# Hybrid decoder trunk on one core: stage boundaries by token blocks, halved norms, an early third gain load, a 512-column first gather and a turned dense product

## What is computed

```
for layer in range(2):
    h = rmsnorm(x, ln1_g[layer])
    a_u, a_b, a_c, s_u, q, k, v, qi, ki, wi, gates = split_columns(h @ w_in[layer])
    y_a = short_conv_mixer(a_u, a_b, a_c, conv_w[layer]) @ w_out_a[layer]
    y_b = s5_mixer(s_u, ...) @ w_out_b[layer]
    y_c = dsa_mixer(q, k, v, qi, ki, wi, ...) @ w_out_c[layer]
    g = sigmoid(gates)                       # three gates of width 1024
    mixed = g[0] * y_a + g[1] * y_b + g[2] * y_c
    x = x + mixed @ w_o[layer]
    h2 = rmsnorm(x, ln2_g[layer])
    x = x + (swiglu(h2, w1, w3, w2) if layer == 0 else moe_ffn(h2, router_w, w1, w3, w2))
```

## Time and profile before

| | us |
|---|---|
| median of 3 runs | 1764.49 (1762.76 to 1767.69) |
| time of the profiled execution | 1763.59 |
| its span from first to last instruction | 1761.8 |
| PE busy | 1687.8 (96%) |
| DVE busy | 1369.3 (78%) |
| ACT busy | 1061.5 (60%) |
| POOL busy | 427.0 (24%) |

### The profile page before, as it was taken

The page is one execution under the profiler, slowest core; times in us unless marked ns, Lnnn a source line. Parts: engine busy times, 40 slices in busy tenths (PEclk is TensorE's granted clock), DMA queues, the critical chain, the costliest instruction groups (busy, mean ns, idle before and its releaser), DMA issues.

```text
span 1761.8 us, 24272 instructions
## 1 busy us (share of the span) xinstructions
PE 1687.8 (96%) x8960; PEld 1431.0 (81%) x8960; DVE 1369.3 (78%) x1135; ACT 1061.5 (60%) x860; POOL 427.0 (24%) x537
## 2 busy tenths in 40 slices
PE   7899998999979999979999999999999999999998
PEld 5887877999868878768888888888888888888886
DVE  6989575454459886558888888888888888888887
ACT  5443455544343544437777777777777777777775
POOL 8979400999024352020000000000000000000200
PEclk9999999999989999979999999999999999999999
DMA  9433365556443343638999999999999999999995
GB/s 326 122 118 116 125 203 176 178 192 200 152 156 121 117 149 129 206 119 293 389 358 388 370 378 386 370 369 382 371 373 378 375 374 389 362 382 369 385 395 193
DMA packets 212425, 481.53 MB, mean 273 GB/s; under 512 B 7904, under 2 KB 32608, under 8 KB 212112
## 3 DMA queue, kind: packets, MB, share of 16 engines
q1 hardware_dynamic: 207456, 463.34, 73.7%
q0 software_dynamic: 4480, 16.78, 2.6%
q10 hardware_dynamic: 432, 0.65, 0.1%
HBM read 473.40 MB, written 7.34 MB: 273 GB/s over the span
## 4 chain that ended last, share of the span: by engine, by line
PE 85%; DVE 10%; ACT 2%; issue 1%; DMA 1%; DVEq 0%; SPq 0%; ACTq 0%; POOLq 0%
PE ps L632 25%; PE ps L634 25%; PE ps L633 25%; DVE w_lo L277 3%; PE ps L1086 1%; PE ps L656 1%; PE ps L657 1%; PE ps L658 1%; ACT w_hi L272 1%; PE ps L755 1%; PE ps L780 1%; PE ps L698 1%; PE ps L782 1%; PE ps L757 1%; DMA raw<-w_in 1%
## 5 line engine op out<-in xcount | busy, mean ns | idle before, releaser
L277 DVE TENSOR_TENSOR w_lo<-raw,w_hi 128x2048 fp32r<-128x2048 f32 (+1 forms) x439 | 1012.1, 2313 | 271.0 <-ACT w_hi L272 269.8
L272 ACT ACTIVATE w_hi<-raw 128x2048 fp32r<-128x2048 f32 (+1 forms) x439 | 839.4, 1914 | 418.7 <-PE ps L634 399.8
L632 PE MATMUL ps<-w_hi,xg_hi 128*128 128x512 f32 x896 | 355.9, 397 | 1.8 <-issue 1.4
L634 PE MATMUL ps<-w_hi,xg_lo 128*128 128x512 f32 x896 | 350.2, 391 | 0.0
L633 PE MATMUL ps<-w_lo,xg_hi 128*128 128x512 f32 x896 | 349.7, 390 | 0.0
L632 PE MATMUL ps<-w_hi,hT_hi 128*128 128x256 f32 (+2 forms) x672 | 229.0, 341 | 2.2 <-DVE hT_lo L1627 2.2
L633 PE MATMUL ps<-w_lo,hT_hi 128*128 128x256 f32 (+2 forms) x672 | 225.3, 335 | 0.0
L634 PE MATMUL ps<-w_hi,hT_lo 128*128 128x256 f32 (+2 forms) x672 | 225.0, 335 | 0.0
L632 PE MATMUL ps<-w_hi,hidT_hi 128*128 128x512 f32 x536 | 209.7, 391 | 3.0 <-DVE hidT_lo L1949 3.0
L634 PE MATMUL ps<-w_hi,hidT_lo 128*128 128x512 f32 x536 | 208.8, 390 | 0.0
L633 PE MATMUL ps<-w_lo,hidT_hi 128*128 128x512 f32 x536 | 208.6, 389 | 0.0
(11 more groups left out here) (357 smaller groups left out, 2046.4 us busy)
## 6 DMA issues: line engine op xcount, KB each, us to landing
raw<-moe_w SPq DMA_DIRECT2D x336, 1024.0 KB, 7.2
raw<-w_in SPq DMA_DIRECT2D x44, 1024.0 KB, 5.5
raw<-ffn_w SPq DMA_DIRECT2D x33, 1024.0 KB, 5.2
raw<-w_o SPq DMA_DIRECT2D x8, 1024.0 KB, 4.9
...
```

What stands on the lines that cost most here:

```text
L272: act.activation(w_hi[:, n % SPLIT, 0:width], raw[:, n % RAW, 0:width], ACT.Copy).then_inc(hi_done, 1)
L277: dve.tensor_tensor(w_lo[:, n % SPLIT, 0:width], raw[:, n % RAW, 0:width], w_hi[:, n % SPLIT, 0:width].bitcast(F32), ALU.subtract).then_in ...
L632: pe.matmul(dst, x_hi, hi, start=first, stop=False, skip_group_check=True)
L634: return pe.matmul(dst, x_lo, hi, start=False, stop=last, skip_group_check=True)
```

## The change

1. **Token blocks at the stage boundaries.** Turned banks now hold one token block and four channel tiles each (`turned_ps`), so a block's bank is complete without the other block. `w_o` is worked as: chunk 0 for block 0, transposes of `mixed` block 1, chunk 0 for block 1, chunk 1 whole, then `two_rows`: the last two chunks for block 0, then for block 1 by column halves. PE turns `mixed` block 0 ahead of the last quarter. Norm steps 1 to 3 run through `enter`: block 0 complete ahead of block 1, and the second of the two early chunk splits moves behind them. The turned banks are 4 to 7 where the addition reads 0 to 3 and the reverse. C_KV goes to banks 4 and 5, with its first half by blocks.
2. **Norm by halves.** Additions, squares and scales work on 512 columns. A dummy root (`root_table`) loads its table before the norm's first square.
3. **Third norm's weights.** Gain 2 is loaded into `su` after the last merge of mixer 0, no longer into `gate` at norm 2.
4. **First gather.** 8 matmuls of 512 columns bring expert 0's rows into `xg_tok`, 8 transposes turn them, in two halves, with copies by ACT and DVE between.
5. **Dense product turned.** `up` has weight tiles stationary and 256 tokens moving, so `hid` comes out turned; `turn_hidden` is gone, and `hid` is split from SBUF. The last stripe's split goes to `h_hi`/`h_lo`, and its `rows` joins `two_rows`. The loop's last pair is written out. The four clearing matmuls of banks 4 to 7 come after the first `up`.

The core of the diff (a line of "..." where lines are left out):

```diff
+        def turned_ps(bank, b, half):
+            return ps[:, bank + 2 * b + half, :].rearrange("p (k n) -> p k n", k=4)
...
+            def two_rows(n, xs, bank, parts, second_ready=None):
+                tile = lambda n, k, h: lambda w: slot_view(w, n, (2, D))[:, k, h * HALF:(h + 1) * HALF]
+                for i, (x_hi, x_lo, k0) in enumerate(xs):
+                    if i == 1 and second_ready is not None:
+                        pe.wait_ge(S["hidT_lo_done"], second_ready)
+                    pe.wait_ge(lo_done, n + i + 1)
+                    for k in range(2):
+                        for h in range(2):
+                            mm = three(ps[:, bank + h, :], x_hi[:, k0 + k, 0:P], x_lo[:, k0 + k, 0:P], n + i,
+                                       tile(n + i, k, h), False, i == 1 and k == 1)
+                mm.then_inc(parts, 1)
+                for h in range(2):
+                    for i, (x_hi, x_lo, k0) in enumerate(xs):
+                        for k in range(2):
+                            mm = three(ps[:, bank + 2 + h, :], x_hi[:, k0 + k, P:SEQ], x_lo[:, k0 + k, P:SEQ], n + i,
+                                       tile(n + i, k, h), False, i == 1 and k == 1)
+                        if h == 1:
+                            mm.then_inc(used, 1)
+                        elif i == 1:
+                            mm.then_inc(parts, 1)
...
+            def turn_block(src, b, bank, ready, seen, done):
+                for k in range(KD):
+                    if k % 4 == 0:
+                        pe.wait_ge(ready, seen + k // 4)
+                    at = (k % 4) * P
+                    tr = pe.transpose(ps[:, bank + 2 * b + k // 4, at:at + P], src[:, b, k * P:k * P + P], ident[:, :])
+                    if k % 4 == 3:
+                        tr.then_inc(done, 1)
+            def norm_turn(i, b, bank):
+                turn_block(h_tok, b, bank, S["h_done"], 4 * i + 2 * b + 1, S["hT_ps"])
...
+            def out_quarters(n, k0, x_hi, x_lo, layer):
+                pe.wait_ge(lo_done, n + 1)
                 for b in range(BLOCKS):
-                    for k in range(KD):
-                        if k % (KD // parts) == 0:
-                            pe.wait_ge(ready, seen + parts * b + k // (KD // parts) + 1)
-                        at = (k % 2) * SEQ + b * P
-                        tr = pe.transpose(ps[:, bank + k // 2, at:at + P], src[:, b, k * P:k * P + P], ident[:, :])
-                        if b == BLOCKS - 1 and k % 2:
-                            tr.then_inc(done, 1)
-            def norm_turn(i):
-                turn_rows(h_tok, 0, S["h_done"], BLOCKS * i, S["hT_ps"])
+                    tok = slice(b * P, b * P + P)
+                    for h in range(2):
+                        for k in range(2):
+                            mm = three(ps[:, 2 * b + h, :], x_hi[:, k0 + k, tok], x_lo[:, k0 + k, tok], n,
+                                       lambda w: slot_view(w, n, (2, D))[:, k, h * HALF:(h + 1) * HALF], False, k == 1)
+                        if (b, h) == (1, 1):
+                            mm.then_inc(used, 1)
+                        else:
+                            mm.then_inc(S["ob_quarters"], 1)
+                        if (b, h) == (1, 0):
+                            turn_block(mixed, 0, 4, S["mixed_done"], 5 * layer + 2, S["mixT_ps"])
...
+                columns_block(c0 + C_KV, 4, 0, 4, KV_W, 0)
+                if layer == 1:
+                    norm_turn(2, 1, 0)
+                    turn_b(1)
+                pe.wait_ge(S["hT_lo_done"], 8 * layer + 3)
+                columns_block(c0 + C_KV, 4, 0, 4, KV_W, 1)
...
+                rows_block(c0 + C_WO, 0, hT_hi, hT_lo, 0, True, False)
+                turn_block(mixed, 1, 4, S["mixed_done"], 5 * layer + 4, S["mixT_ps"])
+                pe.wait_ge(S["mixT_lo_done"], 4 * layer + 3)
+                rows_block(c0 + C_WO, 0, hT_hi, hT_lo, 1, True, False).then_inc(used, 1)
+                rows(c0 + C_WO + 1, 2, hT_hi, hT_lo, False, False)
+                pe.wait_ge(S["mixT_lo_done"], 4 * layer + 4)
+                two_rows(c0 + C_WO + 2, ((hT_hi, hT_lo, 4), (hT_hi, hT_lo, 6)), 0, S["x_parts"])
...
+                        hi, lo = (slot_view(w, n + which, (KD, DENSE_W)) for w in (w_hi, w_lo))
                         for k in range(KD):
                             if i is None and which == 0 and k == KD // 2:
                                 pe.wait_ge(S["hT_lo_done"], 8)
-                            for b in range(BLOCKS):
-                                tok = slice(b * P, b * P + P)
-                                mm = three(ps[:, bank, b * DENSE_W:(b + 1) * DENSE_W], hT_hi[:, k, tok],
-                                           hT_lo[:, k, tok], n,
-                                           lambda w: slot_view(w, n + which, (KD, DENSE_W))[:, k, :],
-                                           k == 0 and b == 0, k == KD - 1)
+                            for c in range(DENSE_W // P):
+                                dst = ps[:, bank, c * SEQ:(c + 1) * SEQ]
+                                cols = slice(c * P, (c + 1) * P)
+                                pe.matmul(dst, hi[:, k, cols], hT_hi[:, k, :], start=k == 0 and c == 0, stop=False,
+                                          skip_group_check=True)
+                                pe.matmul(dst, lo[:, k, cols], hT_hi[:, k, :], start=False, stop=False,
+                                          skip_group_check=True)
+                                mm = pe.matmul(dst, hi[:, k, cols], hT_lo[:, k, :], start=False, stop=k == KD - 1,
+                                               skip_group_check=True)
...
+                norm_turn(1, 0, 4)
+                norm_turn(1, 1, 4)
+                pe.wait_ge(S["hT_lo_done"], 7)
+                up(n0, None, 0)
                 pe.wait_ge(S["zero_made"], 1)
                 clear(4, 4)
...
+                stripe(pairs - 1, 0)
+                up(n0 + 5, DENSE_STRIPES - 1, pairs - 1)
+                pe.wait_ge(S["hidT_lo_done"], DENSE_STRIPES - 1)
+                two_rows(n0 + DENSE_CHUNKS - 2, ((x_hi, x_lo, 0), (last_hi, last_lo, 0)), 4, S["x_parts"],
+                         DENSE_STRIPES)
...
+                def first_gather():
+                    pe.wait_ge(S["pick_done"], BLOCKS)
+                    for half in range(2):
+                        cols = slice(half * HALF, (half + 1) * HALF)
+                        for b in range(BLOCKS):
+                            for src in (h_hi, h_lo):
+                                mm = pe.matmul(ps[:, 2 + half, :], pick[:, b, :], src[:, b, cols],
+                                               start=b == 0 and src is h_hi, stop=b == 1 and src is h_lo,
+                                               skip_group_check=True)
+                        mm.then_inc(S["first_rows"], 1)
+                    for k in range(KD):
+                        if k % 4 == 0:
+                            pe.wait_ge(S["first_taken"], k // 4 + 1)
+                        tr = pe.transpose(ps[:, 6 + k // 4, (k % 4) * P:(k % 4) * P + P],
+                                          xg_tok[:, k * P:k * P + P], ident[:, :])
+                        if k % 4 == 3:
+                            tr.then_inc(S["gather_ps"], 1)
...
+            def root_table():
+                act.wait_ge(S["consts"], 1)
+                act.activation(norm_ss[:, 6, 0:1], ones[:, 0:1], ACT.Sqrt)
...
+                    root_table()
+                    norm(2, 0)
+                    turned_hi(2, 0, S["hT_ps"], 0, S["hT_hi_done"])
+                    norm(2, 1)
                     sp(1)
-                    norm(2)
...
                 split_hi(act, n)
+                root_table()
+                norm(1, 0)
+                turned_hi(1, 0, S["hT_ps"], 4, S["hT_hi_done"])
+                norm(1, 1)
                 split_hi(act, n + 1)
-                norm(1)
...
+                def made_hi(i, rows_used):
+                    act.wait_ge(S["hid_done"], i + 1)
+                    if rows_used is not None:
+                        act.wait_ge(used, rows_used)
+                    act.activation(hidT_hi[:, :], hid[:, :], ACT.Copy).then_inc(S["hidT_hi_done"], 1)
...
+            def enter(i, bank, after, gains, turned_bank):
+                add(i, 0, 0, bank)
+                add(i, 0, 1, bank)
+                variance(i, 0)
+                scale(i, 0, gains)
+                add(i, 1, 0, bank)
+                add(i, 1, 1, bank, after)
+                turned_lo(i, 0, S["hT_hi_done"], turned_bank, S["hT_lo_done"])
+                variance(i, 1)
+                scale(i, 1, gains)
+                turned_lo(i, 1, S["hT_hi_done"], turned_bank, S["hT_lo_done"])
...
+                merge_last(layer, 0)
+                merge_last(layer, 1)
+                merge_last(layer, 2)
+                turned_lo(layer, 0, S["mixT_hi_done"], 4, S["mixT_lo_done"])
+                merge_last(layer, 3)
```

(10 more changed lines are left out.)

363 lines of the change are left out of this document (204 added, 159 removed).

## The result

The changed kernel takes **1746.41 us** (median of 4 runs, 1745.96 to 1747.2) against 1764.09 for the kernel before, run beside it (4 runs). The ratio is 0.9897, 95% interval 0.9885 to 0.9909. The prediction was 1745, range 1738 to 1753. The profiled execution took 1746.7 us, 16.9 less than the one of before.

The account below looks back on a forecast made before the run. PE, busy 96% of the span, was taken as the bound, so only its idling, turning or half clock could be won. Terms summed to -19.2 from 1763.6, giving 1744.4; with 0.9 for the median, 1745 us, range 1738 to 1753.

Parts of the forecast that it names:

- The turned product: Dense FFN: same matmul rate, removed transposes save 3.8 us in the steady loop, 0.9 in the first stripe, 2.0 at the end.
- The clock term of the entry: Entry into the dense FFN after the first norm: some half clock now lies over product, +0.6 us, between 0 and 1.7.
- The merges: End of each mixer: new order loses 0.6 us each; 1.4 given back in layer 1 for half clock; sum -0.2.
- Norm 1: Entry into the dense FFN: block 0 is ready when PE ends its product, gain 2.05 us.
- norm 2: Entry into mixer 1: early gain row and C_KV's start by blocks gain 8.8 us, between 4.3 and 9.5.
- norm 3: Ahead of routing, to the logits' copy: gain only 0.3 us, as the moved chunk split and two `h_lo` stand between.
- Table loads: Norms: the early root puts loads before the squares, in idle time; at the kernel's start 0, between -0.6 and +1.3 us.
- The gather: First gather, before the experts: halves gain 2.3 us; PE starting nearer the low-clock stretch costs +0.6 (0 to 1.2).
- (a): Rival: four or five more half-clock stretches on product, over two merges and three norm entries, giving 1753 us; chance 0.13.
- (b): Rival: ACT or DVE order eats the overlap; of norms 1 to 3 only the gain row's 4.3 us is left, 1752; chance 0.08.
- (c): Rival: the turned dense product runs slower because weight loads show between matmuls, 1770 to 1787 us; chance 0.03.
- (d): Rival: the gain row or freed transposes were hidden anyway, nothing moves by over 5 us, 1761 us; chance 0.04.

Follow-up runs that it names:

- the one just told: Changed kernel with four edits (low half before weight split, chunk 32 behind merge, shifted count, early squares): 1734.96 us, ratio 0.9829 to the kernel before.
- the single edit: Kernel before, with only the third norm's weights loaded early, into `su` behind the last merge of mixer 0: 1760.75 us, ratio 0.9976.

## Why the prediction was right, and where it was wrong

**The bound.** "What is won ahead of the experts arrives at the end unreduced" held: the experts' time lies between 970.9 and 971.6 in nine profiles in which their first product runs at full clock, whatever came before; the tenth is the one just told. (One of the nine has the shorter period.)

**The turned product.** -3.8 -0.9 -2.0 = -6.7 was near on the kernel before (-6.6, with 1.7 of unplanned waits in it), and its rate was 286 ns as before. In the changed kernel the dense product won 3.0. The step that failed is "`hidT_lo` has a whole `up` (11.5 us) to arrive; 0". The product it feeds is late if the low half is, and the low half has not a whole `up`: on DVE it stands behind the split of chunk m+1, which itself waits for ACT's part. And it now reads two SBUF tiles, where the form before read one PSUM bank and one tile. All instructions of the two forms (ns min, median, max): those of the kernel before in its dense stage, eight of which overlap one of POOL's longer instructions, then those of the changed kernel in the experts and in the dense stage:

```profile
L1949 DVE TENSOR_TENSOR hidT_lo<-ps,hidT_hi x11: 676/682/692, 314.2 to 480.6; 128x512 fp32r<-128x512 f32 x11
...
L2109 DVE TENSOR_TENSOR hidT_lo<-ps,hidT_hi x56: 682/684/687, 789.5 to 1730.1; 128x512 fp32r<-128x512 f32 x56
L2118 DVE TENSOR_TENSOR hidT_lo<-hid,hidT_hi x10: 684/980/1757, 313.8 to 471.0; 128x512 fp32r<-128x512 f32 x10
```

I had costed the edit by its place on PE and by the duration of the PSUM form. Together with the half clock behind the wait it gave back 3.5 to 4.3 us. The clock term of the entry was too small besides: half clock lay over 3.8 us of the first product (from 289.99 to 293.8) against 0.7 before, 1.5 us and not 0.6. The Trainium skill has the rule that would have warned me, in "SBUF — State Buffer", SBUF: two separate sides: a VectorE instruction with two SBUF inputs and a GpSimd instruction that reads SBUF share a port pair under an exclusive lock, and the later one blocks until the first is done. The trace agrees: the split that began at 362.56 beside POOL's 362.28 to 364.20 took 1.48 more than 2.29.

**The merges.** Right in kind, +0.8 instead of +0.6 each. What the plan took as given, that DVE comes to the first quarter from a chunk split, was worth 2.7 a merge to change. The half-clock stretch of the earlier trace rows cost 1.5 and not 1.7 (27.75 against 26.25). The -1.4 of clock for merge 1 came, and merge 0 got the same stretch in its place: "I give this back at 8 in 10" treated as a property of the pause what the profiles of one and the same code show to be about even odds (7 of 16). That it came for merge 1 was luck.

**Norm 1** (-2.0 for -2.05), **norm 2** (-9.2 for -8.8, split as the plan had it into weights and order) and **norm 3** (-0.2 for -0.3) were right. C_KV's second chunk began at 492.50, right behind its `w_lo`, 9.4 after the end of the dense product, as the plan had it. At norm 1 one detail was wrong: in this profile ACT's chunk split did not stand in the way of block 1's copy, which waited for PE's transposes at half clock instead. The two were equally long. With the transposes at full clock norm 1 takes 6.8, so its -2.0 is -2.4 in four profiles of nine.

**Table loads.** That they are hidden was right; that it is the early root that hides them was not. The price that the Trainium skill gives ("ScalarE: Activation LUTs", What ACT_TABLE_LOAD costs) was not borne out: no drain stands beside the 1.28, the square root follows it at once (281.35 in the profile without the early root).

**The gather.** -2.4 for -2.3. The clock term of +0.6 was wrong in sign: with the shorter gather the full clock was back ahead of the experts. Before, half clock lay over their first 3.9 us, which cost 1.9; 0.7 of that went again with the extra register value, so the experts show -0.8. In the routing the kernel before had the better draw: PE was now at half clock from 761.5, over its small products, which took 1.2 more.

**The rivals.** (a) was in part what happened (the stretches of merge 0 and of the dense loop, 3.1 us, were beyond my count), made up for by stretches that went elsewhere: in all, half clock lies over some 17 us of product in either kernel's profile. (b), (c) and (d) fell, (b) to the stage table, (c) to the 286 ns and (d) to the single edit's -4.1.

**The signs.** One sign of being right is missing: PE's wait for scaled rows is 16.9 and not below 15. And two of the three signs of being wrong are there: the dense product is 3.0 us shorter and not 6, for the reasons above (if that is what "between its entries" means), and half clock lies on more than 10 us of product. The second says little, since the kernel before has as much. So the time was foretold better than the way to it, and the agreement to 1.4 us is luck in part.
